# A six-layer transformer step in one kernel: query norms as the scale of the exponential, the low-rank layer's pieces in another order, a layer norm in two fused passes

## The reference

```
# gating layer (gmlp)
z = h @ w_in                                  # 1024 u | 1024 v | 512 memory queries
u, v = gelu(z[:, :2048]) in halves
v = (v - mean) * rsqrt(var + eps) * g + b     # layer norm over 1024
mixed = tril(w_s[g]) @ v[group g] + b_s       # 8 groups of 128 columns
mix = u * mixed
# low-rank layer (mla)
z = h @ w_in                                  # 512 cq | 256 ckv | 64 k_rope | 512 memory queries
q = rms(cq) @ w_q_up                          # 8 heads of 128 + 64
k_nope, v = rms(ckv) @ w_kv_up                # 8 heads of 128 and 128
q = rms(q); k = rms([k_nope, k_rope]); rotate the last 64 columns of both
mix = causal softmax(q k^T / sqrt(192)) v
# both layers: 4 heads of 128 against 256 memory keys
q_mem = rms(q_mem)
mem_out = softmax(q_mem k_mem^T / sqrt(128)) v_mem
x = x + [mix, mem_out] @ w_out
x = x + experts(rms(x))
```

## Time and profile before

| | |
|---|---|
| median of 3 runs | 2504.88 us (2504.0 to 2508.75) |
| profiled execution, its own time | 2498.88 us |
| its span in the profile | 2497.1 us |
| PE busy | 2342.5 us, 94% |
| DVE busy | 1519.3 us, 61% |
| ACT busy | 1269.1 us, 51% |
| POOL busy | 85.5 us, 3% |
| DMA | 457.18 MB, mean 183 GB/s |

### The profile page before, as it was taken

How to read it: one execution, slowest core, us unless ns; L and a number is a source line. 1 busy time by engine, 2 the same in 40 slices (tenths; PEclk the granted TensorE clock), 3 DMA queues, 4 the chain that set the end, 5 groups by cost and what they waited for, 6 DMA issues and landing times.

```text
span 2497.1 us, 30867 instructions
## 1 busy us (share of the span) xinstructions
PE 2342.5 (94%) x11269; PEld 1939.7 (78%) x11269; DVE 1519.3 (61%) x1945; ACT 1269.1 (51%) x1739; POOL 85.5 (3%) x173
## 2 busy tenths in 40 slices
PE   7898999999999999998999887999998878999998
PEld 6787888878888788887788766888787757788787
DVE  5765555455556555576554564657887644647887
ACT  5464444454444444455444434546775544446775
POOL 2200000000000000010000020000000200000000
PEclk9999999999999999999999999999999989999999
DMA  7512554525554455550355540657997310657996
GB/s 231 172 35 83 187 191 164 184 85 174 191 189 170 153 194 182 181 182 8 119 190 183 191 142 18 236 186 268 361 368 277 129 51 17 219 185 260 358 365 246
DMA packets 222111, 457.18 MB, mean 183 GB/s; under 512 B 16168, under 2 KB 122956, under 8 KB 221996
## 3 DMA queue, kind: packets, MB, share of 16 engines
q1 hardware_dynamic: 221484, 455.23, 52.5%
q0 software_dynamic: 448, 0.41, 0.1%
q10 hardware_dynamic: 64, 0.02, 0.0%
HBM read 454.55 MB, written 1.05 MB: 182 GB/s over the span
## 4 chain that ended last, share of the span: by engine, by line
PE 74%; DVE 10%; ACT 7%; DMA 6%; issue 3%; POOL 0%; SPq 0%; DVEq 0%; ACTq 0%; POOLq 0%
PE bank L872 16%; PE bank L874 16%; PE bank L873 16%; DVE tail L1845 5%; PE bank L958 3%; PE bank L962 3%; PE bank L960 3%; ACT head L1394 3%; DMA raw<-in_moe_w_down_dram 3%; PE bank L1040 3%; PE bank L1022 2%; DMA raw<-in_moe_w_up_dram 2%; PE bank L1328 2%; PE bank L1330 2%; PE bank L1332 2%
## 5 line engine op out<-in xcount | busy, mean ns | idle before, releaser
L1845 DVE TENSOR_TENSOR tail<-raw,head 128x2048 fp32r<-128x2048 f32 (+4 forms) x267 | 605.3, 2268 | 302.6 <-ACT head L1394 301.7
L1394 ACT ACTIVATE head<-raw 128x2048 fp32r<-128x2048 f32 (+4 forms) x267 | 501.1, 1877 | 235.9 <-PE bank L874 146.2
L872 PE MATMUL bank<-head,xh 128*128 128x512 f32 (+3 forms) x1512 | 593.5, 393 | 25.4 <-DVE xl L1914 13.5
L874 PE MATMUL bank<-head,xl 128*128 128x512 f32 (+3 forms) x1512 | 585.6, 387 | 0.0
L873 PE MATMUL bank<-tail,xh 128*128 128x512 f32 (+3 forms) x1512 | 585.2, 387 | 0.0
L1998 DVE TENSOR_TENSOR tail<-raw,head 128x2048 fp32r<-128x2048 f32 x120 | 275.1, 2293 | 196.6 <-ACT head L1523 196.6
L872 PEld LDWEIGHTS bank<-head,xh 128*128 128x128 f32 x1512 | 286.4, 189 | 83.0 <-issue 13.7
L874 PEld LDWEIGHTS bank<-head,xl 128*128 128x128 f32 x1512 | 285.9, 189 | 56.4
L873 PEld LDWEIGHTS bank<-tail,xh 128*128 128x128 f32 x1512 | 286.7, 190 | 53.4
L1523 ACT ACTIVATE head<-raw 128x2048 fp32r<-128x2048 f32 x120 | 230.1, 1917 | 100.9 <-PE bank L962 100.9
L872 PE MATMUL bank<-head,slot_xh 128*128 128x512 f32 x640 | 256.7, 401 | 2.3 <-DVE tail L1845 1.3
(11 more groups left out here) (372 smaller groups left out, 2731.3 us busy)
## 6 DMA issues: line engine op xcount, KB each, us to landing
raw<-in_moe_w_gate_dram SPq DMA_DIRECT2D x98, 512.0 KB, 4.7
raw<-in_moe_w_up_dram SPq DMA_DIRECT2D x98, 512.0 KB, 6.0
raw<-in_moe_w_down_dram SPq DMA_DIRECT2D x92, 512.0 KB, 5.5
raw<-in_ffn_w_gate_dram SPq DMA_DIRECT2D x88, 512.0 KB, 3.7
raw<-in_ffn_w_up_dram SPq DMA_DIRECT2D x88, 512.0 KB, 4.6
raw<-in_ffn_w_down_dram SPq DMA_DIRECT2D x88, 512.0 KB, 3.9
side<-in_moe_w_down_dram SPq DMA_DIRECT2D x36, 512.0 KB, 5.3
side<-in_moe_w_gate_dram SPq DMA_DIRECT2D x30, 512.0 KB, 5.0
```

Source lines behind the costliest of these rows:

```text
L872: nc.tensor.matmul(y, x0, cols(head), start=start, stop=False)
L874: return nc.tensor.matmul(y, x1, cols(head), start=False, stop=stop)
L1394: nc.scalar.activation(head[:, n % RING, 0:width], raw_at(n)[:, 0:width], ACT.Copy).then_inc(head_made, 1)
L1845: nc.vector.tensor_tensor(tail[:, s, 0:width], raw_at(n)[:, 0:width], head[:, s, 0:width].bitcast(F32), ALU.subtract).then_inc(tail_made, 1)
```

## The change

**Scores.** The jobs of the memory and low-rank heads carry a `scale`: the exponential takes the query's inverse root as its scale, and the maximum is multiplied by it too, one more small VectorE instruction per unit. No engine multiplies the queries any more; GpSimd keeps only the inverse roots. Jobs of the other layers have no scale and run as they did.

**Gating layer.** The layer norm becomes four `scalar_tensor_tensor` passes on VectorE (`(v - mean) * g`, then `* rstd + b`, one row tile each), put between the two pieces of the memory queries' chunk. The flips of the memory queries, their squares and variance go between the two pieces of the first u chunk. The memory attention starts in banks 3, 0, 2 without waiting for the last u chunk and the products u times mixed; these come in its first turns.

**Low-rank layer.** The `w_in` chunks are columns 512 to 831, 0 to 511, 832 to 1343; two of the three flips of the latents, their statistics and the keys' rotation go between the last chunk's two pieces. Then come the keys of all heads (two chunks; the transfer picks 128 of every 256 columns), three chunks of queries, and two of values. Flips follow in four groups, one behind each of the last four chunks. Rotated queries of odd heads get a tile of their own, `rope_odd`, with zeros in the other half, so that one flip is copied out twice with the two columns of `parity`. The squares of the memory queries move into turns 1 and 2 of the attention. `step_ahead` goes. The deferred heads run in turns 4 and 6 on ScalarE, the tails in turns 5 and 7 on VectorE.

```diff
-                    e["gemm_in"](a["a_w_in_2"][0], 0, KD, [(2048, 512)], zdst)
-                    e["gmlp_queries"]()
-                    e["gemm_in"](a["a_w_in_2"][0], 0, KD, [(0, 512)], zdst, gelu=True)
+                    e["gemm_in"](a["a_w_in_2"][0], 0, KD, [(2048, 512)], zdst, between=lambda: e["gmlp_values"]())
+                    e["gemm_in"](a["a_w_in_2"][0], 0, KD, [(0, 512)], zdst, gelu=True, between=lambda: e["gmlp_queries"]())
...
-                    e["gemm_in"](a["b_w_in_2"][0], 0, KD, [(0, 512), (512, 512), (1024, 320)], zdst)
-                    e["prep"](lambda t, k: z[:, t, k * P:(k + 1) * P], 6, G_CQ, "z")
-                    e["stats"](lambda t: z[:, t, 0:512], 512)
-                    e["stats"](lambda t: z[:, t, 512:768], 256)
+                    def latents():
+                        e["prep"](lambda t, k: z_src(t, 4 + k), 2, G_CQ + 4, "z", first=8)
+                        e["prep"](z_src, 2, G_CQ, "z", first=10)
+                        e["stats"](lambda t: z[:, t, 0:512], 512)
+                        e["stats"](lambda t: z[:, t, 512:768], 256)
+                        e["mla_key_rope"]()
+                    w_in = a["b_w_in_2"][0]
+                    e["gemm_in"](w_in, 0, KD, [(512, 320)], zdst)
+                    e["gemm_in"](w_in, 0, KD, [(0, 512)], zdst)
+                    e["gemm_in"](w_in, 0, KD, [(832, 512)], zdst, back=3, between=latents)
+                    e["prep"](lambda t, k: z_src(t, 2 + k), 2, G_CQ + 2, "z", first=12)
...
+                    for f in range(2):
+                        keys_or_values(0, f)
+                        e["mla_key_squares"](f)
                     for f in range(3):
...
+                        queries(f)
+                        e["mla_queries"](f)
+                    for f in range(2):
+                        keys_or_values(1, f, defer=True)
+                        e["mla_flips"](f)
...
+                            if unit[t]["scale"]:
+                                act.wait_ge(head_rstd, unit[t]["scale"][2])
                             nc.scalar.activation(probs(u)[:, lo:hi], score_bank(part, u)[:, at:to], ACT.Exp,
+                                                 scale=scale_of(unit[t], t) if unit[t]["scale"] else 1.0,
...
+                        if unit[0]["scale"]:
+                            link(ins)
+                            dve.wait_ge(head_rstd, unit[0]["scale"][2])
+                            both = negmax[:, 2 * u % 8:2 * u % 8 + 2]
+                            nc.vector.tensor_tensor(both, both, scale_pair(unit[0]), ALU.mult).then_inc(max_ready, 2)
...
+            def gmlp_values():
                 dve.wait_ge(ln_rstd, 1)
                 for t in range(T):
                     v = z[:, t, D:2 * D]
-                    ins = nc.vector.tensor_scalar(v, v, mvar[:, t, 0:1], lnr[:, t:t + 1], ALU.subtract, ALU.mult)
+                    ins = nc.vector.scalar_tensor_tensor(v, v, mvar[:, t, 0:1], ln_gain, ALU.subtract, ALU.mult)
                 link(ins)
-                v = z[:, :, D:2 * D]
-                nc.vector.tensor_tensor(v, v, over(ln_gain, [P, T, D], 1), ALU.mult).then_inc(v_scaled, 1)
+                for t in range(T):
+                    v = z[:, t, D:2 * D]
+                    ins = nc.vector.scalar_tensor_tensor(v, v, lnr[:, t:t + 1], ln_bias, ALU.mult, ALU.add)
+                ins.then_inc(v_normed, 1)
...
-                attend("mla", heads_of_mla() + scores_of_memory(), {3: deferred_step, 5: deferred_step})
+                attend("mla", heads_of_mla() + scores_of_memory(7),
+                       {3: memory_variance, 5: deferred_step, 7: deferred_step})
...
-                q = z[:, :, 2048:2560].rearrange("p t (n d) -> p t n d", d=MEM_D)
-                r = rsh[:, 0:T * MEM_H].rearrange("p (t n) -> p t n", t=T)
-                nc.gpsimd.tensor_tensor(q, q, over(r, [P, T, MEM_H, MEM_D], 3), ALU.mult).then_inc(queries_ready, 1)
-                pool.wait_ge(v_scaled, 1)
-                v = z[:, :, D:2 * D]
-                nc.gpsimd.tensor_tensor(v, v, over(ln_bias, [P, T, D], 1), ALU.add).then_inc(v_normed, 1)
```

415 lines of the change are left out of this document (230 added, 185 removed).

## The result

The changed kernel takes 2464.38 us, the median of four executions (2461.69 to 2465.63), against 2506.82 for the kernel before (four executions, 2504.00 to 2509.21): a ratio of 0.983, 95% interval 0.9813 to 0.9847, 42.4 us. The forecast was 2474 us in a range of 2466 to 2488: right in direction, too small in size.

What follows compares the result with a forecast made beforehand. TensorE, busy 94% of the span, was bounded by its waits (34 us) and the half-speed clock after them. Gating layer 10.9, low-rank layer 11.1 and attention 8.7 sum to 31 us: 2504.9 - 31 = 2474 us, range 2466 to 2488.

Steps and rivals of the forecast that it cites:

- the 3.20 us: TensorE's wait before the first memory scores in the gating layer; at most 2.6 us of it can go.
- the second term: Gating layer: gain from the 3.20 us wait before the first memory scores, taken as 1.3 us, between 0 and 2.6.
- 0.35, 3.5, 0.5 with 1.95, 3.7 and 1.5: TensorE's waits laid out for the new low-rank layer up to its attention, together 11.5 us.
- the 6.0 us between the profiled execution and the median: Last step: the median before lies 6.0 above the profiled execution, so 2504.9 - 31 = 2474 us.
- Of the remaining 44.9 us some 6 are half speed: Low-rank attention before, 50.4 us less two waits of 5.55: some 6 us are half speed after those waits.
- The first rival: Clock still falls in the attention, or VectorE's low-rank queue is longer: 5 to 10 us back, 2479 to 2484; 25%.
- twice 0.45 and 0.4: Low-rank attention: ScalarE's head delays the copy of probabilities about 0.45 us two times; moved squares cost 0.4 once.
- No wait of over 1 us: Sign: the low-rank attention in about 42 us, without such a wait and with no stretch under clock 0.9.
- No other layer changes its instructions: Outside the gating and low-rank layers nothing changes except one tiny pass at the start, costed at nothing.
- The picked transfers: Rival: keys' and values' 128-column pieces land late; slower only from some 16 us a piece, 2514 at 18 us; slower 3%.
- any wait for a root: Rival: multiplied maxima and scaled exponential could hold exponentials back for the inverse root; priced at nothing.
- more goes than I allow: Rival: all three parts at their upper bounds, 12 + 12.7 + 11 = 36 us, 2469; 8%.

Runs made afterwards that it cites:

- gating_alone: The kernel before with the new gating layer alone, low-rank layer as before: 2494.97 us against 2505.32, ratio 0.9962.
- same_turn: The changed kernel with the deferred heads back in the turns of their tails (3 and 5 on both engines): 2468.90 us, 4.5 slower.
- no_chunk_wait: The changed kernel without TensorE's wait for the last `w_in` chunk's copies ahead of the third latent flip: 2464.37 us.
- long_wait: The changed kernel with two extra VectorE passes ahead of the last flips' copies, lengthening TensorE's wait before the low-rank attention: 2468.64 us, 4.3 slower.
- longer_wait_rope64: The changed kernel with five extra VectorE passes ahead of the last flips' copies and the scores' rotated part in 64-row products: 2479.81 us.
- before_short_wait: The kernel before with the keys' norm of heads 4 to 7 left out, shortening TensorE's 5.53 us wait: 2489.89 us against 2505.86, ratio 0.9940.
- rope64: The changed kernel with the rotated part of the low-rank scores back in 64-row products: 2467.54 us against 2464.38, 3.2 slower.
- second profile of before: The kernel before, unchanged, run and profiled again: 2504.93 us (12 executions), ratio to its neighbours 1.0005; the profile's span is 2504.4 us.
- before_rope128: The kernel before with the rotated part of the low-rank scores over all 128 rows, without the zeros: 2493.66 us against 2505.86, ratio 0.9955.

## Why the forecast fell short

**The gating layer: right in size, partly by luck.** 10.9 us forecast, 9.7 to 10.3 measured. VectorE's passes went as laid out, from 1449.4 to 1454.4 at 1.24 us each (the kernel after runs 2.4 us ahead here, which puts the 1451.9 of the forecast at 1449.5). VectorE's copy of the queries' chunk ended at 1457.3, where 1457.6 was laid out, and its copy of the flips at 1460.7 waited only for TensorE's flip. The mixing began at 1465.2 and ran at full clock: up to the last u product the layer gained 10.1 us on the first profile of before, where 9.6 was forecast. Of the 3.20 us almost nothing was left: the first exponential costs a wait of 1.4 us, the first copy of probabilities 1.2 where it was 0.3, and in the profile of after the clock falls for 5 us (0.66) behind the memory attention, about 1.1 us. So the second term, put at 1.3, was 0.1 here, and 1.3 in the profile of `gating_alone`, which has no such dip.

**The low-rank layer to its attention: right.** 11.1 forecast, 10.6 to 11.8 measured; the first score comes 77.5 us behind the layer's first product (1921.85), where 78.2 was laid out and 82 was the bound. The waits came as 0.3, 3.25, 1.0, 3.33 and 1.7 us for 0.35, 3.5, 0.5 with 1.95, 3.7 and 1.5, together 9.6 for 11.5. TensorE's busy time, clock dips included, was 68.0 where 65 and 1.6 had been set, so the two misses cancel in part. That the clock dips for 5 us behind the wait of 3.33 (0.68 from 1978.7 to 1984.0) was in the sum.

**The failed step: the 6.0 us between the profiled execution and the median, and the terms of the attention.** In the terms of the profiled execution the sum came out nearly right: 2468 forecast, 2465.63 measured, and the attention took 40.1 us up to its last transposes where 41.7 was forecast. That is 10.3 us less than in the first profile of before, but 15.8 less than in an ordinary execution (8.7 forecast). Of the 9.6 us between 2474 and 2464.38, 7.2 come from the step to the median. Four things were wrong, in order of size:

- *The base.* "Of the remaining 44.9 us some 6 are half speed" is true of the one execution and not of the kernel: the ordinary one has a mean clock of 0.63 over 39.45 us in the heads' stretch where the one had 0.83 over 33.80 (some 18 us more at the lower level, an estimate from these two), and is 5.7 us longer there. Then the last step, "the median before lies 6.0 above that execution", carried the 6 us over as if they were a constant. They were mostly time that this change takes away: the profiled execution of after lies 1.2 us above its median. The first rival looked for a falling clock after the change only; that the clock before was better than usual in the profile was not asked, although the 6 us between it and every timed run stood in the table.
- *The scores.* I left their cost alone. 64-row products became 128-row products with zeros, 1.48 us a unit instead of 2.16, 5.5 us over eight units. The change's text shows it; the trace of before showed it too, as products of 128 rows and of 64 rows, each 0.63 us apart, where 256 columns at full clock are 0.43 as I had used it for the mixing.
- *ScalarE's copies.* Forecast at 1.3 us (twice 0.45 and 0.4), found at 5.2 us, waits of 2.23, 1.53 and 1.47. A whole head (1.9 us) in a turn that is now 2.5 us of TensorE's work, or eight squares in two turns, are not hidden. "No wait of over 1 us" was wrong. These 3.9 us more took back most of what the scores gave; that the two left out terms nearly cancel, and the sum for the profiled execution came out within 2.4 us, is luck.
- *The stretch taken as untouched.* "No other layer changes its instructions" is not so: the heads and tails of the low-rank layer's first pieces are made within the experts ahead of it, and their smaller width shortens a wait there by 2 to 3 us.

The head one turn ahead of its tail was right (`same_turn`, 4.5 us). The clock of 1.00 throughout was right for the profile of after, with some luck: `no_chunk_wait` and `long_wait` show a dip of some 4 us in the same heads. The new multiplication of the maximum takes 0.16 us and the exponentials with a scale per row 0.46 and 0.55 us against 0.37 and 0.46; neither shows as a wait of its own.

**The rivals.** The picked transfers never showed, nor did any wait for a root. The nearest is "more goes than I allow", but not for its reason: only the attention passed its upper bound (15.8 for 11), since that was counted from the fast execution, and the two other parts lie in the middle of theirs. 42 us lie beyond the 36 of that case too.

**What stays open.** The clock falls behind a wait, and how soon it is back differs between executions. With 64-row products it stayed low for 20 us or more in three profiles of kernels with the old low-rank layer and in `longer_wait_rope64`, but was back within some 4 and 7 us behind waits inside the heads in the first profile of before and in `before_short_wait`; in no profile with 128-row products alone did it stay low for more than some 5 us of the heads at a time. So the mixture makes the long stretch likely, and does not decide it alone; shortening the wait ahead removed it as well, in five of eight executions by their clocks. Why a few executions of the kernel before keep the full clock, and why the new kernel with both suspects lost less on the median than in its profile, no run tells.

## To carry to other kernels

Where a profiled execution lies outside the timed ones, take its distance as a question, not as a constant: take a second profile and find the stretch whose clock differs before a change to that stretch is priced. Look also at the last pieces of the layer ahead: work made in advance for the changed layer stands in them. Don't mix 64-row products into a chain of 128-row ones if zeros can fill the rows. And when TensorE's turn gets shorter, check anew what each other engine fits into a turn, and put its extra work behind what TensorE waits for.

## What the runs showed of the hardware

- Alternating 64-row and 128-row float32 products of 256 columns start 0.63 us apart, 128-row ones 0.43 (`rope64` and after); at a granted clock of 0.50 it is 1.15 (second profile of before) and 0.85 us (`before_rope128`).
- In a stretch in which TensorE was busy throughout, the granted clock stayed at 0.50 for 20 and 24 us with the 64-row products in it, behind waits of 5.5 and 7.5 us, and rose within some 5 us without them, behind waits of 5.5 and 8.1 us. With the same code and the same wait of 5.5 us it was back ahead of the heads in one profile of the kernel before.
- The same code behind the same wait of 2.23 us kept a clock of 1.00 in one profile (after) and fell to 0.70 over 5 us in another (`no_chunk_wait`).
- VectorE's passes over 128 x 1024 with two SBUF inputs: 1.24 us each alone, 2.06 beside a GpSimd multiplication of 2.7 us.
- One program: mean granted clocks of 0.972 to 0.982 (once 0.951) and times of 2492.6 to 2511.7 us for the kernel before, 0.985 to 0.987 and 2461.7 to 2465.6 for the kernel after. Two profiles of the kernel before show the difference in the low-clock stretch.
